# Opening by halves, held-back side loads, and an output projection split between two places in a fused three-layer kernel

## The reference, cut to what matters

```
cond = silu(c)
shift, scale, gate = split(cond @ ada_w + ada_b, 3)      # one adaLN, 1024 -> 3 x 1024
h = rms_norm(x, g) * (1 + scale) + shift
proj = h @ w_in                                          # 1024 -> 512 (u_f) + 512 (u_v) + 512 (u_g)
y_f = real(fft2(u_f in 4 groups of 128, over tokens and channels))
conv = depthwise_conv(u_v * sigmoid(u_g), 31 taps) + conv_b
y_c = silu(layer_norm(conv, ln_g, ln_b))
x = x + gate * (concat(y_f, y_c) @ w_out)
```

## Time and profile before

| | us |
|---|---|
| median of 3 runs | 1865.98 (1865.01 to 1868.82) |
| the profiled execution: its own time | 1866.94 |
| its span in the trace | 1865.0 |
| PE busy | 1390.0 (75%) |
| DVE / ACT busy | 432.3 / 231.6 |
| moved by DMA | 638.01 MB, mean 342 GB/s |

### The profile page before, as it was taken

The page is one execution under the profiler, slowest core; times in us unless marked ns, Lnnn a source line. Parts: engine busy times, 40 slices in busy tenths (PEclk is TensorE's granted clock), DMA queues, the critical chain, the costliest instruction groups (busy, mean ns, idle before and its releaser), DMA issues.

```text
span 1865.0 us, 25692 instructions
## 1 busy us (share of the span) xinstructions
PE 1390.0 (75%) x11264; PEld 751.6 (40%) x11264; DVE 432.3 (23%) x966; ACT 231.6 (12%) x480; POOL 25.8 (1%) x46
## 2 busy tenths in 40 slices
PE   6979766657666567889565656656699885899996
PEld 3824432323332234445232323322346642555553
DVE  1562211104000022534000001000116453311112
ACT  2121100001000020422000000000112322100001
POOL 1000000000000000000000000000020000000000
PEclk8988887888898888988787877778899997899998
DMA  9697999999999983957999999999941302599995
GB/s 377 227 377 296 421 425 425 425 424 425 424 427 424 426 326 113 363 222 289 427 424 427 423 425 426 424 427 424 417 145 65 136 14 100 234 422 420 421 421 225
DMA packets 86379, 638.01 MB, mean 342 GB/s; under 512 B 8476, under 2 KB 8476, under 8 KB 40192
## 3 DMA queue, kind: packets, MB, share of 16 engines
q1 hardware_dynamic: 82608, 623.76, 81.3%
q0 software_dynamic: 3664, 12.64, 1.9%
HBM read 635.30 MB, written 1.96 MB: 342 GB/s over the span
## 4 chain that ended last, share of the span: by engine, by line
DMA 46%; PE 45%; DVE 5%; ACT 3%; issue 1%; SPq 0%; DVEq 0%; ACTq 0%
PE ps L1850 42%; DMA ring<-in_moe_w_up 30%; DMA ring<-in_moe_w_down 13%; DMA ring<-in_ada_w 3%; PE ps L1853 2%; ACT work L2147 1%; DVE x L2388 1%; DVE tmp L2386 1%; SPq L285 0%; ACT tmp L2147 0%; ACT hT L2147 0%; ACT xn L2147 0%; DVE work L633 0%; DVE work L630 0%; DVE work L1493 0%
## 5 line engine op out<-in xcount | busy, mean ns | idle before, releaser
L1850 PE MATMUL ps<-ring,work 128*32 128x256 f32 (+3 forms) x7760 | 775.1, 462 | 346.7 <-DMA ring<-in_moe_w_gate 166.8
L1850 PEld LDWEIGHTS ps<-ring,work 128*32 128x32 f32 (+2 forms) x7760 | 358.8, 132 | 742.8 <-issue 294.8
L2147 ACT ACTIVATE work<-ps 128x256 f32<-128x256 f32 (+3 forms) x188 | 89.1, 479 | 1282.4 <-PE ps L1850 1027.6
L2521 DVE TENSOR_TENSOR work<-work,ps 128x256 f32<-128x256 f32 x32 | 13.5, 421 | 628.0 <-ACT work L2147 628.0
L1850 PE MATMUL ps<-work 32*128 32x256 f32 (+6 forms) x1034 | 138.0, 444 | 17.4 <-ACT work L2147 15.6
L1850 PEld LDWEIGHTS ps<-work 32*128 32x128 f32 (+3 forms) x1034 | 84.2, 205 | 71.1 <-issue 49.4
L1850 PE MATMUL ps<-ring,condT 128*32 128x512 f32 x576 | 81.4, 696 | 23.1 <-DMA ring<-in_ada_w 15.4
L1850 PE MATMUL ps<-ring,hT 128*128 128x512 f32 (+1 forms) x224 | 93.3, 578 | 2.6 <-issue 1.5
L1853 PE MATMUL ps<-const,work 128*128 128x128 f32 (+1 forms) x394 | 66.8, 302 | 22.7 <-ACT work L2147 7.4
L1850 PE MATMUL ps<-work,xn 128*128 128x128 f32 (+2 forms) x416 | 67.8, 315 | 7.0 <-DVE work L1685 6.8
L1853 PEld LDWEIGHTS ps<-const,work 128*128 128x128 f32 (+1 forms) x394 | 49.6, 167 | 56.9 <-issue 23.4
(11 more groups left out here) (300 smaller groups left out, 677.1 us busy)
## 6 DMA issues: line engine op xcount, KB each, us to landing
ring<-in_moe_w_gate SPq DMA_DIRECT2D x64, 2048.0 KB, 16.9
ring<-in_moe_w_up SPq DMA_DIRECT2D x64, 2048.0 KB, 18.4
ring<-in_moe_w_down SPq DMA_DIRECT2D x128, 1024.0 KB, 16.0
ring<-in_moe_w SPq DMA_DIRECT2D x102, 1024.0 KB, 10.7
ring<-in_ada_w SPq DMA_DIRECT2D x72, 1024.0 KB, 11.2
ring<-in_w_in SPq DMA_DIRECT2D x10, 1024.0 KB, 17.1
ring<-in_fc_w_in SPq DMA_DIRECT2D x6, 1024.0 KB, 26.6
ring<-in_attn_w_qkv SPq DMA_DIRECT2D x6, 1024.0 KB, 16.7
```

Source lines behind the costliest of these rows:

```text
L1850: return pe.matmul(out, lhsT, rhs, start=start, stop=stop, skip_group_check=True)
L2147: return nc.scalar.activation(out, in_, f, **kw)
L2521: v.tensor_tensor(hid, act, ps[:, 5, 0:SEQ], ALU.mult).then_inc(S("hid_ready"), 1)
```

## The change

- **The opening goes by halves.** SP loads x and the constants first. Blocks 0 and 1 are no longer shift and scale: "half n" holds columns 512 n to 512 n + 512 of both shift and scale (`first_pieces`), so that after half 0 the features 0 to 511 can be scaled. The first piece of the input projection lies between the halves. x is transposed in two halves (`turned_half`). The 4 wide pieces of the projection are used as piece 0, half 1, pieces 1 to 3, then block 2, then u_f.
- **Side loads held back**: POOL waits for 9 used pieces in place of 6.
- **Blocks**: 3 is between the Fourier stages, 4 and 5 follow; 6 and 7 take the places of 8 and 9 in MoE A's start; 8 is loaded after MoE A's weights and used around the transposes ahead of attention; 9, 10, 11 lie in the rotation of k and q; 12 to 15 in the first four head groups.
- **Output projection**: the matmuls of the Fourier features (`out_rows`) lie before, between and behind the layer norm's two sums; the rest is done token tile by token tile, and DVE updates tile 0 while PE does tile 1.
- Before MoE A the ring now carries 42 pieces, where it carried 50; from there to MoE B 50, where it was 42.

```diff
-P_FC_IN = P_ADA + 8
-P_ADA_1 = P_FC_IN + 6
-P_FC_OUT = P_ADA_1 + BODY
+P_FC_IN = (P_ADA + 4, P_ADA + 9, P_ADA + 10, P_ADA + 11)
+P_ADA_1 = P_ADA + 12
+P_FC_FOURIER = P_ADA_1 + 4
+P_FC_OUT = P_FC_FOURIER + 2 + 12
...
-P_QKV = P_MOE_A + E * 12
+P_ADA_8 = P_MOE_A + E * 12
+P_QKV = P_ADA_8 + 4
@@ attention, PE
+            as_columns(8)
+            ada_block(9)
             for T in range(NT):
                 pe.wait_ge(S("k_rotated"), T + 1)
...
+            as_columns(9)
             for T in range(NT):
+                ada_block(10 + T)
                 pe.wait_ge(S("q_rotated"), T + 1)
...
+                as_columns(10 + T)
...
-                if g < 6:
-                    ada_block(10 + g)
+                if g < 4:
+                    ada_block(12 + g)
@@ SP
-            ada_pieces(0)
+            def first_pieces(v):
+                w = rows_of(A["ada_w"][0, 0])
+                for q in range(4):
+                    c0 = D * (q % 2) + 512 * v
+                    stream(ada_at(v) + q, w[:, 4 * (q // 2):4 * (q // 2) + 4, c0:c0 + 512])
...
             sp.dma_start(x[:, :, :], ...)
             sp.dma_start(const[:, :], ...)
-            ada_pieces(1)
-            wide_pieces(P_FC_IN, A["fc_w_in"][0], HALF)
-            half_pieces(P_FC_IN + 4, A["fc_w_in"][0], 0)
-            for g in range(2, 8):
+            first_pieces(0)
+            conv_piece(0)
+            first_pieces(1)
+            for kp in range(1, 4):
+                conv_piece(kp)
+            ada_pieces(2)
+            half_pieces(P_FC_FOURIER, A["fc_w_in"][0], 0)
+            for g in range(3, 6):
                 ada_pieces(g)
             plain_pieces(P_FC_OUT, A["fc_w_out"][0])
...
-            for g in range(8, 10):
+            for g in range(6, 8):
                 ada_pieces(g)
             experts(P_MOE_A, 0)
+            ada_pieces(8)
@@ POOL
-            pool.wait_ge(S("piece_used"), 6)
+            pool.wait_ge(S("piece_used"), P_ADA + 9)
@@ PE, opening
+                ada_piece(0, 0)
                 pe.wait_ge(S("dealt_ready"), 1)
+                pe.wait_ge(S("xn_act"), 1)
+                pe.wait_ge(S("xn_dve"), 1)
+                turned_half(0)
+                for kp in range(1, 4):
+                    ada_piece(0, kp)
+                turned_half(1)
+                as_columns(0)
+            def fourier_conv():
+                for kp in range(4):
+                    if kp % 2 == 0:
+                        pe.wait_ge(S("hT_dve"), 2 + kp)
+                        pe.wait_ge(S("hT_act"), 2 + kp)
+                    loaded(pe, P_FC_IN[kp])
...
+                        if k == 2:
+                            as_columns(1)
+                    last.then_inc(S("piece_used"), 1)
+                    if kp == 0:
+                        ada_block(1)
+                ada_block(2)
...
+                def out_rows(kp, kk):
+                    n = P_FC_OUT + kp
+                    loaded(pe, n)
+                    k = 2 * kp + kk
+                    for T in range(NT):
+                        for h in range(2):
+                            last = mm(ps[:, 2 * T + h, :], ycat[:, k, P * T:P * T + P],
+                                      slot(n)[:, D * kk + 512 * h:D * kk + 512 * h + 512], k == 0, False)
+                    if kk:
+                        last.then_inc(S("piece_used"), 1)
+                pe.wait_ge(S("row_copied"), 6)
+                pe.wait_ge(S("yf_ready"), 2)
+                out_rows(0, 0)
+                as_columns(5)
+                out_rows(0, 1)
                 pe.wait_ge(S("conv_ready"), 1)
...
-                ada_block(6)
+                out_rows(1, 0)
                 pe.wait_ge(S("sq_ready"), 1)
...
-                ada_block(7)
-                as_columns(7)
+                out_rows(1, 1)
                 gate_row(0, 0)
                 pe.wait_ge(S("yc_ready"), 4)
-                project_out(P_FC_OUT, ycat)
+                for T in range(NT):
+                    for kp in (2, 3):
...
+                        if T:
+                            last.then_inc(S("piece_used"), 1)
+                    if T == 0:
+                        last.then_inc(S("out_ps"), 1)
@@ PE, before attention
-            transposed_norm(2, 2)
+            pe.wait_ge(S("filter_out"), 15)
+            for kp in range(3):
+                ada_piece(8, kp)
+            transposed_norm(2, 2, 0)
+            ada_piece(8, 3)
@@ ACT, mixer
+                ada_rows(2)
...
+                ada_rows(3)
...
-                for g in range(2, 6):
+                for g in range(4, 6):
                     ada_rows(g)
+                table_for(ACT.Sqrt)
                 sc_.wait_ge(S("centred"), 1)
                 act_(sq, cv, ACT.Square).then_inc(S("sq_ready"), 1)
-                ada_rows(6)
-                table_for(ACT.Sqrt)
@@ DVE, mixer
-                dve.wait_ge(S("piece_used"), P_FC_OUT + 4)
-                update_x(lambda T: ps[:, 2 * T:2 * T + 2, :])
+                dve.wait_ge(S("out_ps"), 1)
+                update_x(lambda T: ps[:, 2 * T:2 * T + 2, :], P_FC_OUT + 4)
```

More of the change, by code:

```diff
@@ L296, in ada_at @@
         def ada_at(g):
-            for first, n in ((16, P_TAIL_B), (10, P_ADA_2), (8, P_TAIL_A), (2, P_ADA_1), (0, P_ADA)):
+            for first, n in ((16, P_TAIL_B), (9, P_ADA_2), (8, P_ADA_8), (6, P_TAIL_A), (3, P_FC_FOURIER + 2),
+                             (2, P_ADA_1), (1, P_ADA + 5), (0, P_ADA)):
                 if g >= first:
@@ L1786, in experts @@
                             load(sp, n, down[:, 0, kp])
-            for g in range(8, 10):
+            for g in range(6, 8):
                 ada_pieces(g)
             experts(P_MOE_A, 0)
+            ada_pieces(8)
             wide_pieces(P_QKV, A["attn_w_qkv"][0])
             half_pieces(P_QKV + 4, A["attn_w_qkv"][0], D)
-            for g in range(10, 16):
+            for g in range(9, 16):
                 ada_pieces(g)
@@ L1936, in project_out @@
                     last.then_inc(S("piece_used"), 1)
[L1938 to L1946, removed]
+            def fourier_conv():
[4 more added lines that the diff above has]
+                    loaded(pe, P_FC_IN[kp])
+                    w = slot(P_FC_IN[kp]).rearrange("p (k f) -> p k f", k=2)
+                    for kk in range(2):
+                        k = 2 * kp + kk
+                        for f in range(8):
+                            last = mm(ps[:, f // 2, SEQ * (f % 2):SEQ * (f % 2) + SEQ],
+                                      w[:, kk, P * f:P * f + P], hT[:, k, :], k == 0 and f % 2 == 0, k == KD - 1)
+                        if k == 2:
[4 more added lines that the diff above has]
+                ada_block(2)
+                pe.wait_ge(S("mod_copied"), 2)
+                for q in range(2):
+                    loaded(pe, P_FC_FOURIER + q)
+                    w = slot(P_FC_FOURIER + q).rearrange("p (k f) -> p k f", k=4)
+                    for kk in range(4):
+                        k = 4 * q + kk
+                        for f in range(4):
+                            last = mm(ps[:, 4 + f // 2, SEQ * (f % 2):SEQ * (f % 2) + SEQ],
                                       w[:, kk, P * f:P * f + P], hT[:, k, :], k == 0 and f % 2 == 0, k == KD - 1)
                     last.then_inc(S("piece_used"), 1)
[L1950 to L1953, removed]
                 pe.wait_ge(S("phase_const"), 16)
@@ L1973, in fourier_conv @@
                     last.then_inc(S("yf_ps"), 1)
-                pe.wait_ge(S("glu_ready"), 1)
-                for g in range(2, 6):
+                for g in range(4, 6):
                     ada_block(g)
+                    as_columns(g - 1)
+                def out_rows(kp, kk):
+                    n = P_FC_OUT + kp
+                    loaded(pe, n)
+                    k = 2 * kp + kk
+                    for T in range(NT):
+                        for h in range(2):
+                            last = mm(ps[:, 2 * T + h, :], ycat[:, k, P * T:P * T + P],
+                                      slot(n)[:, D * kk + 512 * h:D * kk + 512 * h + 512], k == 0, False)
+                    if kk:
+                        last.then_inc(S("piece_used"), 1)
@@ L2088, in experts @@
                     if e == 1:
-                        pe.wait_ge(S("mod_copied"), 2 + late + 2 - 8)
+                        pe.wait_ge(S("mod_copied"), copied(late + 1))
                     if e:
@@ L2173, in adaln @@
                 table_for(ACT.Sigmoid)
-                ada_rows(0)
-                ada_rows(1)
+                for n in range(2):
+                    ada_rows(n)
+                    sc_.wait_ge(S("gain_ready"), n + 1)
+                    sc_.wait_ge(S("hT_ps"), 2 * n + 2)
+                    for j in (4 * n + 2, 4 * n + 3):
+                        act_(hT[:, j, :], ps[:, 5 + 2 * n, SEQ * (j % 2):SEQ * (j % 2) + SEQ], ACT.Identity,
+                             scale=gain[:, 0, j:j + 1], bias=mod[:, 0, j % 4, n, 0:1]).then_inc(S("hT_act"), 1)
```

(20 more changed lines are left out.)

140 lines of the change are left out of this document (85 added, 55 removed).

## The result

The changed kernel takes **1837.67 us** (median of 4 runs, 1836.73 to 1838.47), against 1867.22 us (1865.01 to 1868.82) for the kernel before: ratio 0.9842, 95% interval 0.9825 to 0.9859. The gain is 29.5 us. The forecast was 1831, a gain of 35; the time lies in the range of 1823 to 1841. The profiled execution took 1838.14 us, its span is 1836.0, 29.0 less than before. One execution of all those reported here, of the kernel with the larger side loads held until u_f is used, took 7007.91 us, and it is left out of that kernel's ratio.

What follows compares the result with a forecast made beforehand. MoE A is bound by its DMA weight stream, which starts at M, so time won before it counts whole: 1866.9 - 37.2 (M) + 2 (attention) = 1831.7, or 1830.8 against the median, said as 1831; range 1823 to 1841.

Steps and rivals of the forecast that it cites:

- a shift ahead of MoE A comes through whole: MoE A's weight stream ends a fixed time after it begins, so an earlier start counts in full: 37.2 us.
- M: Start of MoE A's first block, behind the output projection: forecast to move from 177.30 to 140.1, bounds 138 and 147.
- the opening: Start to sigmoid: first projection matmul at 24.6 against 38.18, sigmoid at 58.8 against 67.75.
- PE at the sums: Mixer, ahead of the layer norm's sums: PE ready at 110.8, half a microsecond behind the convolution's end at 110.3.
- without that cover it costs up to 2: Side loads among block 2 and u_f, 2.9 MB or 7 us: nothing charged, up to 2 on PE if weights come late.
- the forecast's 410: DMA rate in GB/s for plain pieces in the opening, one every 2.56 us.
- third rival: PE not at the sums in time, two `out_rows` (7.2) on the path: 1838, chance 0.05.
- attention: First scores 6.1 later from blocks in k's and q's rotation, 4.0 back in head groups: net +2.1, taken as +2.
- the low clock that could cost +11: Rotation of k and q: if the hole stays at 1.2 GHz, blocks and rows cost up to 9 more.
- The 4.0 from the two lighter head groups: Attention: two of the last head groups lose their block, steps of 6.8 in place of 8.8.
- the rival's "Against: DMA share 0.19 there": Rotation of k and q: moved blocks cost more through low clock or late weights, attention +9, 1838.7, chance 0.13.
- The -1: Attention, if denser work keeps PE at 2.4 GHz: first scores and block shorten by 3, time 1828.7.

Runs made afterwards that it cites:

- the version with M 15.2 later: Against the changed kernel, no output matmul before y_c is ready, all 32 in one run behind it: 1852.96 us, ratio 0.9904 to the kernel before.

## Why the prediction was right, and where it was off

**Right: a shift ahead of MoE A comes through whole.** M to the last down piece took 492.2 for 491.3, at 424 GB/s for 425, and the version with M 15.2 later took 15.3 longer. No modulation transfer stands between the convolution and the output matmuls.

**Right: the opening.** First projection matmul at 24.80 (24.6), sigmoid at 59.07 (58.8), end of the convolution at 110.60 (110.3). These three terms were sums of rows, and they hold to 0.3 us. So close a fit is in part luck: in three other executions of the same opening the sigmoid came at 60.26, 60.27 and 60.56.

**Off: PE at the sums.** The step that failed is "block 2 lands by 57 ..., u_f's pieces by 62, wanted at 62.3 and later. I charge nothing; without that cover it costs up to 2, on PE only". u_f's weights were there at 65.69, a wait of 3.08, and behind it the clock fell (0.66 in 65 to 70), so that its 64 records took 15.74 where they take 14.08. The size that was wrong is the rate: from the first piece's issue at 37.64 to its landing, DMA moved 369 GB/s, 10.3 MB; an estimate from these figures is that the forecast's 410 would have brought them in 25.1 us, by 62.8, about when PE wanted them (62.6). The "without that cover it costs up to 2" was short too, since wait and clock together cost 4.7. The prediction says once that PE is half a microsecond behind the convolution and once that it has half a microsecond of slack; the first follows from its sums, so there was no slack, and nearly all of it went on the path: 4.0 of the 5.3 us by which M was missed. The others: 1.3 for the last matmuls (15.70 for 14.3, clock 0.66) and 0.3 for the opening, less 0.3 between the sums and y_c. The version with u_f first shows that the late weights are the cause at the sums: the wait is gone, PE takes the first sum within 0.1 us of the convolution's end, and M comes to 139.49 and 140.57. It does not show the cause of the 1.3 behind y_c, though these matmuls happened to run at the full clock in it. The prediction had this mechanism as its third rival, at 1838 and with a chance of 0.05; that is what happened, at a smaller price (4.0 later than forecast, for 7.2), with the last matmuls, attention and MoE A adding the rest. That its 1838 is the measured time to half a microsecond is luck. A cover "spent exactly" deserved more than 1 in 20.

**Off, and small: attention.** +3.3 for +2.1. The first scores come 4.5 later behind QKV's end (6.1 forecast), with PE at 1.00: the low clock that could cost +11 did not come, and 1.7 of the 4.5 are waits for weights. The 4.0 from the two lighter head groups came: two steps from 759.27 to 773.13 took 13.9, where the two from 784.50 to 802.33 took 17.8. But first scores to update is only 0.9 shorter (105.5 for 106.4), because the four steps with a block, which the sum had left unchanged, took 43.7 for 42.1, and because the rest behind the lighter steps took 1.5 more (the gate row's matmuls 3.78 for 2.52, at the low clock). The chain of the kernel before in its head steps:

```profile
754.79 6.37 PE ps L1850 x48
...
765.43 8.22 PE ps L1850 x64
...
775.69 6.77 PE ps L1850 x64
...
784.50 4.76 PE ps L1850 x48
```

Its steps were 10.6, 10.3 and 8.8 long, the first two at a low clock (16 records of scores in 1.93 and 2.03 where they take 1.15). In the changed kernel they are 11.2, 10.6 and 9.9, from 727.65 on: the first and the last wait for weights (1.9 and 0.9), the middle one has no such wait and runs at a low clock. So what the fuller PE won by its clock, the weights took: with half of their bytes left out the four steps take 38.7. The failed step is the rival's "Against: DMA share 0.19 there": that share was of a stage that asked for few bytes. Blocks 9 to 15 are 28 pieces, they now come at a stretch, and at 409 GB/s a block takes 10.3 us while a head step with a block takes 8.8 at the full clock. Here the stated sign of failure, a ring wait between QKV and the head groups, appeared.

**The clock.** In the rotation, PE's granted clock rose from 0.64 to 1.00 when work filled the holes, and the first scores took 2.00 where they took 3.79. The Trainium skill's page "TensorE: Matmul & The Clock Gate", part 1, has the slow clock as the default that activity releases; the trace agrees there. The -1 that this would give for attention did not come with all bytes loaded (+3.3); with half of the weights of blocks 10 to 15 left out it was passed, at -3.7 (176.4 for 180.1). Further on, in the head steps without a block, the clock is 0.61 (760 to 790).

**Not counted:** -1.3 behind attention, within the 1012.5 to 1017.0 of the versions, and +0.9 in MoE A, where the versions took 491.5 to 493.1, all a little more than the 491.3 of before; why is not known.

**Left open.** Why DMA moved 369 GB/s and not 410 ahead of u_f: the side loads and the slower rows of the half-width pieces were not separated. The early side loads together with u_f first were not tried.

## What to carry to other kernels

Where two engines meet and the forecast slack is under a microsecond, price the next late transfer as if it will happen, and the clock with it. Move a needed load ahead of a less urgent one rather than holding others back: held back, the same bytes came to lie on another load. And when a stage with holes is filled with work, ask what its weights need per step, since a low DMA share before says only that nobody asked.

## What the runs showed of the hardware that was not expected

- A wait of 3 us in the middle of dense matmuls can be enough for the granted clock to fall. Behind waits of 2.91, 3.08 and 3.47 us for u_f it fell (0.66 in the 5 us from 65, behind the 3.08), and its 64 records took 15.67 to 15.74; behind 0.78, 1.75 and 2.56 it stayed at 1.00 and they took 14.05. A wait of 2.33 us ahead of block 5's last piece, with little PE work before it, did lower it (0.54 in 104.6 to 108, and 5.56 in place of 3.68).
- One and the same idle of 2.48 to 2.49 us ahead of the last output matmuls ended at the lower clock in eight traces (15.47 to 15.70) and at the full clock in two, both of the kernel with u_f first (14.00). With u_f first and the whole opening, where PE did the same work before it, it was the lower clock again; which idle drops the clock could not be told from the traces.
- A transfer's time from issue to landing tells mostly what was in flight with it: u_f's first piece of 1 MB took 27.91 us, but DMA moved 10.3 MB in that time, 2.9 of them side loads, at a share of 1.03 and 369 GB/s. In MoE A a share of 1.01 gave 424 to 425 GB/s.
